# The last x tile inside the first half of the in-projection, and feature-major attention values, in a two-layer mixer step

## What is computed

```
h = modulate(rmsnorm(x, lp['norm_w'][1]), mod[:, 3], mod[:, 4])
...
proj = h @ lp['w_in']
z, xbc, dt_raw, gq, gk, gv, gr, g_lr, aq, ak, av = split_cols(proj, IN_SPLITS)
...
av = av.reshape(Bsz, L, ATT_HEADS, ATT_HEAD_DIM)
att = dilated_attention(aq, k_ctx, v_ctx, k_buf.shape[1], n_abs).reshape(Bsz, L, ATT_DIM).astype(h.dtype)
```

## Time and profile before

| | us |
|---|---|
| median of 3 runs | 2514.59 |
| lowest, highest | 2514.55, 2515.67 |
| the profiled execution, its time | 2517.65 |
| its span in the profile | 2515.9 |
| PE busy in the span | 2439.6 (97%) |
| DVE busy | 1646.5 (65%) |
| ACT busy | 1044.0 (41%) |

### The profile page before, as it was taken

The page is one execution under the profiler, slowest core; times in us unless marked ns, Lnnn a source line. Parts: engine busy times, 40 slices in busy tenths (PEclk is TensorE's granted clock), DMA queues, the critical chain, the costliest instruction groups (busy, mean ns, idle before and its releaser), DMA issues. The chain is left out here.

```text
span 2515.9 us, 49391 instructions
## 1 busy us (share of the span) xinstructions
PE 2439.6 (97%) x19293; PEld 2286.3 (91%) x19293; DVE 1646.5 (65%) x2840; ACT 1044.0 (41%) x1701; POOL 11.4 (0%) x43
## 2 busy tenths in 40 slices
PE   7999999899998999999999999998999999999998
PEld 5998999899976999999999999988989679999997
DVE  7872784564867787278478538736568577855854
ACT  5541452342554454145255325424237435533532
POOL 0000000000000000000000000000000000000000
PEclk8999999999999999999999999999999999999999
DMA  8246336522133224733233553464121332332331
GB/s 298 78 136 220 111 84 196 185 60 84 56 121 101 68 68 123 221 100 95 81 84 84 161 182 100 119 216 130 60 72 51 122 104 64 84 98 79 100 86 61
DMA packets 398244, 285.70 MB, mean 114 GB/s; under 512 B 18273, under 2 KB 396439, under 8 KB 397702
## 3 DMA queue, kind: packets, MB, share of 16 engines
q1 hardware_dynamic: 397676, 283.36, 37.2%
q10 hardware_dynamic: 410, 0.18, 0.0%
HBM read 271.71 MB, written 11.79 MB: 113 GB/s over the span
## 5 line engine op out<-in xcount | busy, mean ns | idle before, releaser
L347 PE MATMUL PS<-f_xH,f_wqH 128*128 128x288 f32 x2224 | 659.2, 296 | 3.1 <-issue 3.0
L347 PE MATMUL PS<-f_xL,f_wqH 128*128 128x288 f32 x2224 | 656.1, 295 | 0.0
L347 PE MATMUL PS<-f_xH,f_wqL 128*128 128x288 f32 x2224 | 654.0, 294 | 0.0
L347 PEld LDWEIGHTS PS<-f_xH,f_wqH 128*128 128x128 f32 x2224 | 416.7, 187 | 5.9 <-issue 5.4
L347 PEld LDWEIGHTS PS<-f_xH,f_wqL 128*128 128x128 f32 x2224 | 418.8, 188 | 0.0
L347 PEld LDWEIGHTS PS<-f_xL,f_wqH 128*128 128x128 f32 x2224 | 417.5, 188 | 0.0
L347 PE MATMUL PS<-f_actH,f_wqH 128*128 128x288 f32 x1408 | 323.7, 301 | 1.3 <-DVE f_wqL L987 1.3
L347 PE MATMUL PS<-f_actH,f_wqL 128*128 128x288 f32 x1408 | 315.3, 295 | 0.0
L347 PE MATMUL PS<-f_actL,f_wqH 128*128 128x288 f32 x1408 | 315.2, 295 | 0.0
L746 DVE SCALAR_TENSOR_TENSOR xT<-PS,modT,xT 128x288 f32<-128x288 f32 (+1 forms) x80 | 41.4, 518 | 366.0 <-PE PS L347 366.0
L347 PEld LDWEIGHTS PS<-f_actH,f_wqH 128*128 128x128 f32 x1408 | 230.1, 189 | 27.0 <-issue 25.0
(11 more groups left out here) (508 smaller groups left out, 4412.0 us busy)
## 6 DMA issues: line engine op xcount, KB each, us to landing
wslot<-in_ffn_w_in SPq DMA_DIRECT2D x176, 512.0 KB, 5.1
masks<-in_w_mod SPq DMA_DIRECT2D x42, 1536.0 KB, 6.7
wslot<-in_ffn_w_out SPq DMA_DIRECT2D x64, 384.0 KB, 4.2
wslot<-in_w_in SPq DMA_DIRECT2D x44, 512.0 KB, 4.8
wslot<-in_ffn_w_out SPq DMA_DIRECT2D x64, 320.0 KB, 3.4
setup<-in_w_mod SPq DMA_DIRECT2D x6, 1536.0 KB, 13.8
wslot<-in_w_out SPq DMA_DIRECT2D x16, 512.0 KB, 4.6
dec<-in_cache_attn_k SPq DMA_DIRECT2D x16, 384.0 KB, 4.8
```

What stands on the lines that cost most here:

```text
L347: ins = e.matmul(outs[j], w, x_hl[j][part], start=(start and w is wh and part == 0), stop=(stop and w is wl), skip_group_check=True)
```

## The change

Two things are changed, and the schedule between them.

**The opening.** On DVE `finish_x` stands after `scale_half(3, 0)`, and `sample_scale` before `low(7, 0)`. On ACT the square of tile 7's second half stands after `high(3)`; the root stays after `high(7)`. On PE `second_sums` stands inside `first_groups(0)`, ahead of tile 6.

**The values.** The two av units are 256 and 128 columns wide and feature-major: 3 groups (14, 15, 16) of 48 matmuls in place of 10 of 24. Each is copied to `vT`, a new pair of buffers in the SSD input's memory, turned by PE in 5 transposes (`turn_v`) into the group's own banks, and copied by ACT to `av` (`keep_v`, two copies). The wait on a kept av group becomes a wait on `v_kept`, for a group two later and for SP's stores of v, POOL's clearing and `values`.

**The schedule.** Levels 5, 6 and 7 stand behind half groups of groups 12 and 13, the GLA chunks behind quarters of group 14, the samples' output and the three turns of v between parts of groups 15, 16 and 17. The next unit's split stands at the end of step 3 in place of step 0.

```diff
-            ("av", O_AV, 192), ("av", O_AV + 192, 192),
+            ("av", O_AV, 256), ("av", O_AV + 256, 128),
...
-        if kind in ("av", "gv"):
+        if kind == "gv":
             out += [(u, kind, "token", t, nth) for t in range(NTT)]
...
+                            if groups[n - 2][1] == "av":
+                                e.wait_ge(sem("v_kept"), 2 * (groups[n - 2][4] + 1))
...
+                    def turn_v(m):
+
+                        n = V_AT + m
+                        b, v = bank_of(n), vT[:, m % 2, :]
+                        e.wait_ge(kept_by[n], kept_no[n])
+                        for c in range(NCH):
+                            e.transpose(PS[:, b, c * P:(c + 1) * P], v[:, c * P:(c + 1) * P], ident[:])
+                        e.transpose(PS[0:TS, b + 1, 0:P], v[:, SEQ:T], ident[:]).then_inc(sem("v_turned"), 1)
...
                             e.wait_ge(sem(q + "h_ready"), lows(kt, h))
+                            if h == 0 and kt == DT - 2:
+                                second_sums(e, q)
...
+                    group(PAIR_AT, 0, 2)
+                    level(NLEV - 3)
+                    group(PAIR_AT, 1, 2)
+                    level(NLEV - 2)
+                    group(PAIR_AT + 1, 0, 2)
+                    level(NLEV - 1)
+                    group(PAIR_AT + 1, 1, 2)
+                    turn_ke()
+                    for c in range(NCH):
+                        group(V_AT, c, NCH)
+                        gla_chunk(c)
+                    group(V_AT + 1, 0, 4)
+                    gla_sample_out()
+                    group(V_AT + 1, 1, 4)
+                    turn_v(0)
+                    group(V_AT + 1, 2, 4)
+                    group(V_AT + 1, 3, 4)
+                    gla_norm_sums()
+                    group(V_AT + 2, 0, 2)
+                    turn_v(1)
+                    group(V_AT + 2, 1, 2)
+                    gla_sample_state()
...
+                        if s == 2:
+                            turn_v(2)
...
+                        if d == 3:
+                            e.wait_ge(sem(q + "x_whole"), 1)
+                            square_half(e, DT - 1, 1).then_inc(sem(q + "last_square"), 1)
...
+                    def keep_v(m):
+
+                        b, r = bank_of(V_AT + m), slice(m * P, (m + 1) * P)
+                        e.wait_ge(sem("v_turned"), m + 1)
+                        e.activation(av[:, 0:NCH, r], PS[:, b, :].rearrange("p (c k) -> p c k", k=P), ACT.Copy)\
+                            .then_inc(sem("v_kept"), 1)
+                        e.activation(av[0:TS, NCH, r], PS[0:TS, b + 1, 0:P], ACT.Copy).then_inc(sem("v_kept"), 1)
...
                     for d in range(1, DT):
                         scale_half(d, 0)
+                        if d == 3:
+                            finish_x(e, q, pending, small[:, 512:512 + TS])
                         low(d - 1, 0)
+                    sample_scale(e, link, 1, s4)
                     low(DT - 1, 0)
-                    finish_x(e, q, pending, small[:, 512:512 + TS])
-                    sample_scale(e, link, 1, s4)
...
-                        if s == 0:
-                            split_ahead(ATT_FROM - 1)
                         if part:
                             keep_group(n)
                             split_ahead(n)
+                        if s == 3:
+                            split_ahead(ATT_FROM - 1)
```

More of the change, by code:

```diff
@@ L100, in projection_groups @@
             continue
-        out += [(u, kind, "feature", c, (c0 // P if kind == "zx" else 2 * nth) + c) for c in range(2)]
+        out += [(u, kind, "feature", c, (c0 // P if kind == "zx" else 2 * nth) + c) for c in range(width // P)]
     return out
@@ L2032, in _ @@
                     first_groups(0)
-                    second_sums(e, q)
                     e.wait_ge(w_split, u_in + 2)
@@ new lines, in _ @@
+                    e.activation(oT[:, :, SEQ:T], PS[:, 6:8, 0:TS], ACT.Copy)\
+                        .then_inc(sem("oT_kept"), 1)
+                    e.wait_ge(sem("oT_kept"), 2)
+                    for p2 in range(2):
+                        e.activation(oroot[p2], oT[:, p2, :], ACT.Square).then_inc(sem("o_squares"), 1)
+                    keep_v(0)
+                    keep_group(V_AT + 1)
+                    split_ahead(V_AT + 1)
+                    for p2 in range(2):
+                        e.wait_ge(sem("o_sumsq"), p2 + 1)
+                        e.activation(halves(oroot[p2]), bank2(4 + 2 * p2), ACT.Sqrt, scale=1.0 / GV, bias=epsc[:])\
+                            .then_inc(sem("o_root"), 1)
@@ L2471, in split_ahead, with level @@
                             split_lo(e, wH, wL, u_in + groups[n][0] + 2)
-                    for n in range(ATT_FROM):
+                    def level(v):
+                        if v + 1 < NLEV:
+                            scaled(v + 1)
+                        if v + 3 < NLEV:
+                            distances(v + 3)
+                        e.wait_ge(sem("lev_scored"), v + 1)
+                        for h in range(GH):
+                            lev_keep(v, h)
+                        if v == 0:
+                            e.wait_ge(sem("kE_exp"), 1)
+                            e.tensor_tensor(kE, kE, gkT, ALU.mult).then_inc(sem("kE_ready"), 1)
+                            e.wait_ge(sem("eG_ready"), 1)
+                            e.tensor_tensor(qE, eG, gqT, ALU.mult).then_inc(sem("kE_ready"), 1)
+                    for n in range(PAIR_AT):
                         keep_group(n)
```

147 lines of the change are left out of this document (64 added, 83 removed).

## The result

The changed kernel took 2502.09 us (median of six executions, 2496.83 to 2502.71) beside 2516.58 for the kernel before: a ratio of 0.9938 over all executions, 95% interval 0.9925 to 0.9951, so 15.6 us faster (the two medians alone differ by 14.5). Two later groups of executions gave 0.9932 (0.9918 to 0.9946) and 0.9926 (0.9911 to 0.9942), 17.1 and 18.6 us. The forecast was 19.6 us, a ratio of 0.9922. The direction was right, and so was the mechanism in its main terms; by the ratios the size was 1 to 4 us too large.

The account below looks back on a forecast made before the run. PE, busy 97% of the span, was taken as the bound. Opening 2.9, values and levels 11.5, `turn_v(2)` -0.9 and step 2 6.1 gave 19.6 us: 2514.59 to 2495.0 us (profiled execution 2498.1), range 2490.5 to 2501.5.

Parts of the forecast that it names:

- The opening: In-projection's start: sums 12 matmuls earlier shorten PE's 3.06 us wait to about 1.5; gain 2.9 us for both layers.
- no wait over 0.3 us inside `first_groups(0)`: Sign expected in the profile after: PE waits no longer than this among the first half's tiles in the opening.
- Values and levels: Groups 12 on: values' PE time 41.6 to 35.3 us, less a 0.5 us wait at level 6; 11.5 us for both layers.
- a rule of the Trainium skill: Isolated matmul costs N / 2.4 + 2.5 ns; the value groups would then gain 2.2 us where the rows give 8.8.
- Step 2: Attention step 2: moving DVE's low part removes PE's 1.67 us wait and 1.41 us of clock; 6.1 us for both layers.
- The clock: Granted clock: 1.41 us a layer gained at step 2; falls behind the opening's wait left at zero, 1.4 us either way.
- The clock falls more often: Rival: remaining waits at other times bring two or three more falls at 1.4 us; about 2498.5 us, chance 0.12.
- The opening's chain: Rival: it does not get shorter because delayed `low` holds PE up as much; 2.9 us left out, 2497.9, chance 0.06.
- the wait at the scores: Rival: step 2's wait survives, on the GLA state's add or `turn_v(2)`; 6.1 us left out, 2501.1, chance 0.08.
- the levels: Rival: DVE does levels 5 to 7 alone, PE waiting about 12.4 us a layer; 2518.8 us, slower, chance 0.01.
- swallowed at the stage's end: Rival: PE finishes earlier but DVE's convolution or an unmoved transfer ends the stage; 2511 to 2515 us, chance 0.05.
- PE pays by columns: Rival: 192 columns cost 192/288 of 288 ones; gain 6.6 us a layer smaller, 2508 us, chance 0.02.

Follow-up runs that it names:

- after_again: The changed kernel run again with nothing edited; median 2498.48 us, ratio 0.9932.
- before_again: The kernel before run again with nothing edited; 2516.29 us, ratio 0.9999.
- values_only: The changed kernel with the opening and the low part at step 2 put back as before; 2500.12 us, ratio 0.9948.
- open_only: The kernel before with the opening's part of the change alone; 2512.95 us, ratio 0.9989.
- late_low_only: The kernel before with only DVE's low part of the unit split ahead of attention step 2 moved to step 3; 2516.42 us, ratio 1.0007.
- norm_late: values_only with DVE's first normalization of the GLA output put behind the last group's copy; 2501.54 us, ratio 0.9939.
- norm_behind: values_only with DVE's first normalization of the GLA output put behind the add of the GLA state; 2507.43 us, ratio 0.9962.
- after_pad2: The changed kernel with 12 more matmuls a layer in the last in-projection group, output the same; 2503.85 us, ratio 0.9959.
- after_pad4: The changed kernel with 24 more matmuls a layer in the last in-projection group, output the same; 2504.46 us, ratio 0.9954.
- after_fill: The changed kernel with four identity transposes on PE in each of two waits of each SSD stage; 2500.17 us, ratio 0.9931.
- tight: The changed kernel with `second_sums` 12 matmuls earlier still and DVE's low part of unit 6 behind level 6; 2494.6 us, ratio 0.9910.

## Why the prediction was right, point by point

**The bound.** That PE's path sets the end of the in-projection held: in layer 0 the opening gave 1.52 us, values and levels 6.0 and step 2 2.71, and the SSD stage began 10.24 us sooner after the in-projection's start.

**The opening.** Forecast 1.6 and 1.3 us. Where the clock fell in the first half, before and after alike, it gave 1.4 to 1.65. In the second layer I allowed 0.25 us for a new wait at tile 2. In the profile `after_again`, without a fall there, it is larger:

```profile
1714.36 0.40 PE L347 MATMUL PS<-mx_hH,in_wH 128*128 128x288 f32 x1 [0.69 <-DVE mx_hL L807]
```

This is `finish_x` on DVE's path, seen at full clock, where the working looked for it, but longer than the 0.25 us allowed; the working's sign of no wait over 0.3 us inside `first_groups(0)` is not kept there. With the clock down in the first half no wait over 0.15 us shows. Against a kernel before that has no fall there either (first matmul to second half 14.44 us in before_again) the gain is 1.1 us (13.33).

**Values and levels.** Forecast 5.75 a layer net; measured 6.0. The piece of 12 at 1.76 against 1.79, the wait at level 6 at 0.46 against 0.5, none at 7. This is the largest term and it was right to 0.3 us. The prediction had set a rule of the Trainium skill against its rows (TensorE: Matmul & The Clock Gate, section "Back-to-back issue gap", the gap of an isolated matmul). By that rule the gain would be 6.6 us a layer smaller, an estimate, and so there would be none; the measured 6.0 us decide for the rows.

**Step 2.** Forecast 3.1 us a layer, less 0.46 for `turn_v(2)`; measured 2.70 together in both layers. The size was right, the cause only half: I put the wait down to the low part alone. It was the low part and the normalization in a row, and values_only shows that the change removed it twice over.

**The clock: the term that does not hold as it was put.** The forecast counted 1.41 us a layer, 2.8 in all, as a gain because the fall behind the wait at step 2 would go. It went, and falls came up elsewhere: in the profiles above the mean clock of the changed kernel (0.986, 0.989, 0.989) is hardly above that of the kernel before (0.985, 0.989). And the fall does not belong to the wait. In the second profile of the kernel before itself, layer 1 has the same wait of 1.67 us with the clock at 1.00 behind it:

```profile
1856.87 0.33 PE L1994 MATMUL PS<-ident,att_prompt 128*128 128x128 f32 x1 [1.67 <-DVE att_prompt L2290]
```

```profile
1857.00:1861.00 4.00, 4.00 (x34) 3.77 (x34) 3.90 (x8) 1.18 (x5) 0.00 (x0) 1.00 0.88 272
```

In open_only it is so in both layers. Timeline of PE, then the clock of layer 0 and of layer 1:

```profile
1851.75 0.33 PE L1994 MATMUL PS<-ident,att_prompt 128*128 128x128 f32 x1 [1.67 <-DVE att_prompt L2296]
```

```profile
623.50:628.00 4.50, 4.48 (x36) 4.25 (x37) 4.36 (x10) 1.53 (x6) 0.00 (x0) 1.00 0.92 277
1850.00:1856.00 6.00, 4.33 (x36) 4.03 (x35) 5.83 (x12) 1.29 (x6) 0.12 (x1) 1.00 0.79 241
```

Without a term for falls that go, the sum is 1.65 (opening) + 6.0 (values) + 1.67 - 0.46 (step 2) = 8.86 us a layer, 17.7 together, and the three comparisons gave 15.6, 17.1 and 18.6. The 1.65 is the opening's gain where the clock is down in the first half before and after; at full clock it is 1.1. The same count for every kernel, against what its ratio makes of 2516 us:

| kernel | count | measured | interval |
|---|---|---|---|
| open_only | 3.3 | 2.8 | 0.3 to 5.5 |
| late_low_only | 3.3 | -1.8 | -4.5 to 0.8 |
| values_only | 14.4 | 13.1 | 9.6 to 16.4 |
| norm_late | 14.4 | 15.3 | 11.6 to 18.9 |
| norm_behind | 10.7 | 9.6 | 6.0 to 12.8 |
| changed | 17.7 | 15.6, 17.1, 18.6 | 12.3 to 22.4 |
| after_pad2 | 14.5 | 10.3 | 6.8 to 13.6 |
| after_pad4 | 11.3 | 11.6 | 8.1 to 15.1 |
| after_fill | 17.7 | 17.4 | 13.8 to 20.9 |
| tight | 20.9 | 22.6 | 18.9 to 26.4 |

(norm_behind has lost 0.18 a layer at step 2 and pays `turn_v(2)`; tight has 3.2 more than the changed kernel by its expectation, and 2.6 to 3.5 in the profiles.) Eight kernels lie within 1.8 us of their count (the changed one by its mean). With the clock's 2.8 us values_only would be counted at 17.2, outside its interval, and the changed kernel at 20.5, above all three of its values, though inside two of its three intervals. Two don't fit: after_pad2, 4.2 us short of its count, and late_low_only, 5 us short. With the opening at 1.1 in both layers (and tight's second step at 0.8 instead of 1.1 a layer) the counts with the opening are 1.1 lower, tight's 1.7; then after_pad2 too lies inside its interval, and late_low_only alone does not. For that kernel the profile shows where one execution lost what was gained (an opening's fall and an SSD stage of 78.1 us), and its lower mean clock over 11 executions accounts for most of the rest; why it falls more often is open.

The counts do not show that the clock gives nothing in all. Over every recorded execution its mean is 0.9872 for the changed kernel (17) and 0.9863 for the kernel before (72), a difference of 0.0010, give or take 0.0009, or some 2.4 us of 2516 as an estimate. So the 2.8 us may have come in part, by falls anywhere in the program. What the runs refute is that a gain of 1.41 us is tied to each wait removed at step 2.

**The rivals.** "The clock falls more often" named what kept the first profiled execution at 2502.71 us, 4.6 over the 2498.1 forecast for it: two or three falls at 1.4 us. It is not a property of the kernel, though: the second and third profiled executions took 2498.12 and 2498.19. That these meet the 2498.1 so closely is luck, since two executions of the kernel before took 2517.65 and 2513.59. The opening's chain did get shorter, the wait at the scores did not survive, the levels cost 0.46 us and not 12, and nothing was swallowed at the stage's end. That PE pays by columns is excluded by the 6.0 us.

## What to carry to other kernels

Cost a removed wait by its own length and leave the clock behind it out of the sum: a fall that goes at one place can come at another, and a single profile can be 4 us off for this alone. Where a wait stands behind two long operations in a row on the same engine, look for both, and for what releases the first of them: handing the copy ahead of them to another engine was worth as much here as moving the second. A stretch that the change leaves alone and that has changed its length says something about the execution; profile the unchanged kernel twice before explaining it.

## What the runs showed of the hardware

The granted clock stayed at the lower level while PE was never idle: in 776 to 784 us of the changed kernel PE is busy for 8.00 of 8.00 us with 103 short matmuls, at 0.57, and PEld for 6.42. Ahead of that fall it had been busy for 6.01 of 6.90 us, with no gap over 0.6 us; in after_fill, where the larger gap is filled, for 6.45 of 6.90, and the clock fell all the same. The stretches, in this order:

```profile
769.40:776.30 6.90, 6.01 (x91) 4.55 (x90) 5.08 (x7) 4.58 (x8) 0.00 (x0) 1.00 0.69 232
```

```profile
769.40:776.30 6.90, 6.45 (x93) 4.90 (x93) 5.08 (x7) 4.29 (x8) 0.00 (x0) 1.00 0.70 232
```

In the in-projection, where both are busy nearly all the time with matmuls of 288 columns, the clock stays at 1.00 (9.86 and 9.62 of 9.90 us). Whether the kind of work makes the difference, or the gap of 0.3 us that is left, was not tried. The same instructions ran at full clock in a second execution of the same program.
